# The first four units of each stage on gain times z instead of on the normalised x, their products ordered by feature block

## The reference

```
h = layer_norm(ALPHA * h + 0.5 * swiglu_ffn(h, w_in, w_out), gain, bias)
h = layer_norm(ALPHA * h + mix(h), gain, bias)
h = layer_norm(ALPHA * h + 0.5 * swiglu_ffn(h, w_in, w_out), gain, bias)

layer_norm(x) = (x - mean(x)) * rsqrt(var(x) + eps) * gain + bias     # over the 1024 features
swiglu_ffn(h) = (silu(h @ w_gate) * (h @ w_up)) @ w_out               # d_ff = 2816
```

## Time and profile before

| | us |
|---|---|
| median of 3 runs | 1088.29 |
| lowest and highest | 1086.24, 1088.48 |
| span of the profiled execution, first to last instruction | 1086.3 |
| TensorE (PE) busy | 1063.5 |
| VectorE (DVE) busy | 693.0 |
| ScalarE (ACT) busy | 510.1 |
| GpSimd (POOL) busy | 178.2 |

### The profile page before, as it was taken

The page is one execution under the profiler, slowest core; times in us unless marked ns, Lnnn a source line. Parts: engine busy times, 40 slices in busy tenths (PEclk is TensorE's granted clock), DMA queues, the critical chain, the costliest instruction groups (busy, mean ns, idle before and its releaser), DMA issues.

```text
span 1086.3 us, 21913 instructions
## 1 busy us (share of the span) xinstructions
PE 1063.5 (98%) x8293; PEld 1035.4 (95%) x8293; DVE 693.0 (64%) x972; ACT 510.1 (47%) x737; POOL 178.2 (16%) x188
## 2 busy tenths in 40 slices
PE   7999999999999999999999999999999999999996
PEld 6999999989999999999899999997998989999995
DVE  5755556588788555565676565658545877666664
ACT  5434344463347343444553434447745665434442
POOL 4000002230062000012400000223131460000032
PEclk9999999999999999999999999999999999999998
DMA  9756555627564765556285555562632528665531
GB/s 260 213 174 173 168 167 169 192 81 213 174 173 113 200 174 173 161 174 183 85 231 175 173 168 161 176 172 81 178 98 78 153 84 242 182 191 170 173 103 40
DMA packets 343692, 175.14 MB, mean 161 GB/s; under 512 B 6658, under 2 KB 342576, under 8 KB 343632
## 3 DMA queue, kind: packets, MB, share of 16 engines
q1 hardware_dynamic: 342992, 173.36, 55.9%
q10 hardware_dynamic: 448, 0.85, 0.2%
q0 software_dynamic: 192, 0.10, 0.0%
HBM read 173.24 MB, written 1.05 MB: 160 GB/s over the span
## 4 chain that ended last, share of the span: by engine, by line
PE 94%; DVE 4%; ACT 1%; DMA 1%; issue 0%; POOL 0%; SPq 0%; DVEq 0%; POOLq 0%; ACTq 0%
PE bank L1089 28%; PE bank L1091 28%; PE bank L1090 28%; PE bank L1109 2%; PE bank L1113 2%; PE bank L1110 2%; DVE rstd L791 1%; DMA raw_weights<-in_ffn_w_in_dram 1%; PE bank L1304 1%; PE bank L1321 1%; DVE scaled L800 1%; DVE weights_lo L734 0%; DVE resid L788 0%; PE bank L1131 0%; PE bank L1317 0%
## 5 line engine op out<-in xcount | busy, mean ns | idle before, releaser
L734 DVE TENSOR_TENSOR weights_lo<-raw_weights,weights_hi 128x1024 fp32r<-128x1024 f32 x335 | 424.8, 1274 | 247.2 <-ACT weights_hi L437 246.4
L437 ACT ACTIVATE weights_hi<-raw_weights 128x1024 fp32r<-128x1024 f32 x337 | 355.2, 1059 | 451.9 <-PE bank L1091 443.9
L1089 PE MATMUL bank<-x_hi,weights_hi 128*128 128x272 f32 (+1 forms) x1640 | 474.5, 289 | 0.5 <-DVE yc_lo L941 0.3
L1091 PE MATMUL bank<-x_hi,weights_lo 128*128 128x272 f32 (+1 forms) x1640 | 472.6, 288 | 0.0
L1090 PE MATMUL bank<-x_lo,weights_hi 128*128 128x272 f32 (+1 forms) x1640 | 471.0, 287 | 0.0
L1089 PEld LDWEIGHTS bank<-x_hi,weights_hi 128*128 128x128 f32 x1640 | 310.4, 189 | 4.5 <-issue 3.5
L1091 PEld LDWEIGHTS bank<-x_hi,weights_lo 128*128 128x128 f32 x1640 | 310.6, 189 | 0.0
L1090 PEld LDWEIGHTS bank<-x_lo,weights_hi 128*128 128x128 f32 x1640 | 310.5, 189 | 0.0
L1089 PE MATMUL bank<-mid_hi,weights_hi 128*128 128x272 f32 (+1 forms) x704 | 201.3, 286 | 0.0
L1091 PE MATMUL bank<-mid_hi,weights_lo 128*128 128x272 f32 (+1 forms) x704 | 201.1, 286 | 0.0
L1090 PE MATMUL bank<-mid_lo,weights_hi 128*128 128x272 f32 (+1 forms) x704 | 200.9, 285 | 0.0
(11 more groups left out here) (169 smaller groups left out, 897.8 us busy)
## 6 DMA issues: line engine op xcount, KB each, us to landing
raw_weights<-in_ffn_w_in_dram SPq DMA_DIRECT2D x176, 512.0 KB, 3.9
raw_weights<-in_ffn_w_out_dram SPq DMA_DIRECT2D x64, 512.0 KB, 4.0
raw_weights<-in_ffn_w_out_dram SPq DMA_DIRECT2D x32, 384.0 KB, 3.4
raw_weights<-in_conv_w_in_dram SPq DMA_DIRECT2D x24, 512.0 KB, 3.9
raw_weights<-in_gla_w_in_dram SPq DMA_DIRECT2D x24, 512.0 KB, 3.8
raw_weights<-in_conv_w_out_dram SPq DMA_DIRECT2D x8, 512.0 KB, 4.0
raw_weights<-in_gla_w_out_dram SPq DMA_DIRECT2D x8, 512.0 KB, 4.0
out_dram<-out_tok SPq DMA_DIRECT2D x3, 256.0 KB, 2.2
```

The lines of the kernel that those rows point to most:

```text
L437: nc.scalar.activation(w_hi[:, n % RING, :], raw[:, n % RING, :], ACT.Copy).then_inc(hi_split, 1)
L734: nc.vector.tensor_tensor(w_lo[:, s, :], raw[:, s, :], w_hi[:, s, :].bitcast(F32), ALU.subtract).then_inc(lo_split, 1)
L1089: nc.tensor.matmul(ps, w_h, hi[:, k, cols], start=first and k == k0, stop=False)
L1091: mm = nc.tensor.matmul(ps, w_l, hi[:, k, cols], start=False, stop=last and k == k1 - 1)
```

## The change

The first four units after a norm (FOLD = 4) no longer use the norm's output, except in f0, which has no norm in front. They multiply `zg = gain * z`, split into zg_hi (ScalarE, `round_raw`) and zg_lo (VectorE, `raw_low`) chunk by chunk during the out-projection. Two more columns of zg hold gain and bias, so each bank also receives w.gain and w.bias. After the norm's statistics VectorE turns each of the four banks into `unfolded` (`unfold`), and the consumer adds `fold_bias`. The mean products stand inside the four units, before block 2. The 96 products run over the blocks outside and the four units inside. `keep_warm` is gone from the boundaries. VectorE's `scaled` is written back into resid and h_f is no longer used for x; all eight residual blocks are made on ScalarE (`take_residual`), all eight are centred on GpSimd. One low split of weights goes between block 5 and 6 of the normalising loop, and in f2 to gla the unfolding of unit 0 goes between block 1 and 2 (`early`). The fifth unit waits for `xlo_ready` block by block.

```diff
+            def round_raw(q, mo, n_tok, step=0):
+                nc.scalar.activation(zg_hi[:, at, cols], resid[:, at, cols], ACT.Identity,
+                                     scale=gain_at(q, step * 2 + mo)).then_inc(zghi_ready, 1)
+            def take_residual(q, k, n_tok):
+                act.wait_ge(xlo_ready, KD * (q + 1) + k + 1)
+                nc.scalar.activation(resid[:, k, cols], resid[:, k, cols], ACT.Identity, scale=ALPHA,
+                                     bias=alpha_bias[:, q * KD + k:q * KD + k + 1]).then_inc(resid_ready, 1)
...
+            def raw_low(q, mo, n_tok, step=0):
+                dve.wait_ge(zghi_ready, step * 2 + (KD * q + mo + 1))
+                nc.vector.scalar_tensor_tensor(out=zg_lo[:, at, cols], in0=resid[:, at, cols],
+                                               scalar=gain_at(q, step * 2 + mo), in1=zg_hi[:, at, cols].bitcast(F32),
+                                               op0=ALU.mult, op1=ALU.subtract).then_inc(zglo_ready, 1)
+            def unfold(q, n0, u, n_tok):
+                dve.wait_ge(unit_used, n0 + u + 1)
+                nc.vector.scalar_tensor_tensor(out=unfolded[:, u, cols], in0=mean[:, cols], scalar=ps[:, n_tok:n_tok + 1],
+                                               in1=ps[:, 0:n_tok], op0=ALU.mult, op1=ALU.subtract,
+                                               reverse1=True).then_inc(fold_step, 1)
+                nc.vector.tensor_copy(fold_bias[:, u:u + 1], ps[:, n_tok + 1:n_tok + 2])
+                dve.wait_ge(fold_step, FOLD * q + u + 1)
+                nc.vector.tensor_tensor(unfolded[:, u, cols], unfolded[:, u, cols], rstd[:, cols],
+                                        ALU.mult).then_inc(fold_ready, 1)
...
+                    if k >= 1:
+                        x_low(k - 1)
+                    if k == 1 and early is not None:
+                        early()
+                    if k == 5:
+                        split_lo(late + RING)
...
+                    unfold(q, n0, 0, n_tok)
+                    unfold(q, n0, 1, n_tok)
+                    split_lo(n0 + RING)
+                    gate_times_up(0)
+                    split_lo(n0 + 1 + RING)
+                    unfold(q, n0, 2, n_tok)
+                    unfold(q, n0, 3, n_tok)
+                    split_lo(n0 + 2 + RING)
+                    gate_times_up(1)
+                    split_lo(n0 + 3 + RING)
...
+            def multiply_raw(n0, q, n_tok):
+                for u in range(FOLD):
                     pe.wait_ge(lo_split, n0 + u + 1)
-                keep_warm(n0, WARM[1])
-                pe.wait_ge(var_ready, q + 1)
-                keep_warm(n0, WARM[2])
-                pe.wait_ge(std_ready, q + 1)
-                keep_warm(n0, WARM[3])
+                pe.wait_ge(fold_cols, 4 * (q + 1))
                 for k in range(KD):
+                    if k == 2:
+                        mean_total(q, n_tok)
+                        mean_squares(q, n_tok)
+                    pe.wait_ge(zglo_ready, KD * q + k + 1)
+                    for u in range(FOLD):
+                        ps = bank[u][:, 0:n_tok + 2]
+                        nc.tensor.matmul(ps, w_h, zg_hi[:, k, cols], start=k == 0, stop=False)
+                        nc.tensor.matmul(ps, w_h, zg_lo[:, k, cols], start=False, stop=False)
+                        mm = nc.tensor.matmul(ps, w_l, zg_hi[:, k, cols], start=False, stop=k == KD - 1)
                         if k == KD - 1:
                             mm.then_inc(unit_used, 1)
+                pe.wait_ge(mean_copied, q + 1)
+                pe.wait_ge(var_ready, q + 1)
...
             for j in range(GLA_TILES):
+                if 0 < j < FOLD:
+                    unfold(FFN_NORM[2], n0, j, T)
                 if j < GLA_TILES - 1:
                     split_lo(n0 + j + RING)
```

More of the change, by code:

```diff
@@ L492, in normalise, with out_projection @@
                     act.dma_start(out[0, P:, D // 2:], out_tok[:, 1, D // 2:]).then_inc(out_stored, 16)
-            def out_projection(q, n0, parts, n_tok):
+                else:
+                    for k in range(KD - 2, KD):
+                        take_residual(q, k, n_tok)
+            def out_projection(q, n0, parts, n_tok, early=None):
                 def chunk(mo, step=0):
@@ L811, in normalise, with out_projection @@
                     x_low(KD - 1)
-                for n in late:
-                    split_lo(n + RING)
-            def out_projection(q, n0, parts, n_tok):
+            def out_projection(q, n0, parts, n_tok, early=None):
                 def chunk(mo, step=0):
@@ L946, in conv_chunk @@
                 split_lo(n + RING, step)
+                if m == 0:
+                    for u in range(1, FOLD):
+                        unfold(FFN_NORM[0], n0, u, T)
                 convolve(m, step)
                 split_lo(n + 2 + RING, step)
+            unfold(FFN_NORM[0], n0, 0, T)
             conv_chunk(0)
@@ L1187, in ffn @@
                 else:
-                    multiply_together([bank[b][:, 0:n_tok] for b in range(4)], n0, q)
+                    multiply_raw(n0, q, n_tok)
                 if q is None:
                     pe.wait_ge(consts_ready, 1)
-                tile(2)
+                tile(2, ready=None if q is None else (xlo_ready, KD * (q + 1)))
                 tile(3)
@@ L1228, in _ @@
             every = slice(0, T)
[L1229 removed]
+            multiply_raw(n0, FFN_NORM[0], T)
             def conv_chunk(m, step=0):
@@ L1234, in conv_chunk @@
                 for part in range(1 if m == 1 else 0, 3):
-                    multiply(bank[3 * (m % 2) + part][:, 0:T], n0 + 3 * m + part, (x_hi, x_lo), every, step=step)
+                    multiply(bank[3 * (m % 2) + part][:, 0:T], n0 + 3 * m + part, (x_hi, x_lo), every, step=step,
+                             ready=(xlo_ready, KD * (FFN_NORM[0] + 1)) if m == 1 and part == 1 else None)
             conv_chunk(1)
@@ L1347, in _ @@
                 cols = main if short else every
-                multiply(bank[j % 2][:, 0:SEQ if short else T], n0 + j, (x_hi, x_lo), cols)
+                multiply(bank[j % 2][:, 0:SEQ if short else T], n0 + j, (x_hi, x_lo), cols,
+                         ready=(xlo_ready, KD * (FFN_NORM[2] + 1)) if j == 4 else None)
                 if j == 4:
```

298 lines of the change are left out of this document (186 added, 112 removed).

## The result

The changed kernel takes 1094.41 us (median of 4 runs, 1093.54 to 1094.82), the kernel before beside it 1088.11 us (4 runs). The ratio is 1.0059, with a 95% interval of 1.0046 to 1.0071: slower by 0.6%. The forecast was 1092.1, slower. The profiled execution has a span of 1092.7 us against 1086.3.

What follows compares the result with a forecast made beforehand. TensorE, busy 1063.5 of 1086.3 us, bounds the kernel, so only its pauses can be won. Terms +3.5 - 2.0 - 2.9 + 6.4 - 1.2 = +3.8 us, added to the 1088.29 median, give 1092.1 us; range 1081 to 1100.

Steps and rivals of the forecast that it cites:

- What is removed: At five norm boundaries: 18 warming products and the norm wait go; four units end at +12.9 instead of +19.1 us.
- VectorE up to the last x block: After a norm, VectorE's scaled blocks and low parts, partly slowed beside GpSimd's centring, deliver block 7 at +17.2 us.
- the first rival: In the sixteen normalising instructions, GpSimd's centring does not hold VectorE: block 7 at +15.1, kernel 1080 us; chance 0.22.
- The first tile: At f1 to f2, the third pair waits for the first gate-times-up: TensorE restarts at +22.2, before +25.1; 2.9 us gained.
- Conv: At f0 to conv, the third chunk waits for yc_lo until +27.6: 1.9 us lost, plus 1.6 of low clock, 3.5 together.
- gla: At f2 to gla, VectorE's wait for unit 0 and unit-by-unit copies and splits lose 6.4 us; bounds 0 and 10.
- The ping-pong of 3.6 us: In gla, units 1 to 3 each take unfold, kT copy, high split and low split in turn, 3.6 us a unit.
- The signs named: New-trace TensorE waits: x_lo 1 to 2 us, mid_lo 1.5, yc_lo near 7, kT near 4; low clock behind conv, gla.
- the 20 below which I would have been wrong: Refutation test: the forecast is wrong if TensorE's waits for VectorE and ScalarE sum to less than 20 us.
- the boundaries behind stages with one unit per block: Conv to f1 and gla to f3: raw_low adds 0.42 to 0.75 us per block; 2.0 and 1.2 us gained.
- the 23.1 and 22.7 of the sum: Forecast TensorE restarts, in us after +0, at conv to f1 and gla to f3, with gains of 2.0 and 1.2.
- The rival with the clock in the feed-forward stages: At the feed-forward boundaries the clock falls too, costing 3 x 1.6 us and the port's 1.4 more: 1098; chance 0.16.

Runs made afterwards that it cites:

- the unit order: The 96 raw products unit by unit instead of block by block: 1095.55 us against the changed kernel's 1094.41; on top of the four changes of order, 1082.65 us.
- the last experiment but one: Changed kernel with four changes of order together (gla unfoldings, conv convolution, late split, early unfolding), plus the 96 products unit by unit: 1082.65 us, ratio 0.9952.
- the first: Changed kernel with only the 96 products unit by unit instead of block by block, mean products after the first unit: 1095.55 us, ratio 1.0077.

## Why the prediction was right

**What is removed.** The raw products start 0.12 us after the last out-projection product at all five boundaries, and at f1 to f2 the four units end near +13.1, forecast +12.9. Right.

**VectorE up to the last x block.** Forecast +17.2, measured +17.4, and GpSimd's centring ends at +11.2 for a forecast of +11.3. Of the durations, three instructions beside GpSimd took 1.02 instead of the 0.85 of the earlier trace rows, and the undisturbed ones followed each other every 0.41 instead of 0.43; the two nearly cancel. Without the centring the last block came at +15.5, where the first rival had +15.1, and the restarts in front of conv and the feed-forward stages moved by the 2 us that it named. The rival priced the disturbance at these four restarts rightly and was wrong that it would be absent. Its 1080 us asked for more: in gla the restart did not move (+33.11), and the slow clock in conv stayed (238.06 to 244.89), so that the run stands at 1087.2.

**The first tile.** Forecast +22.2, measured +22.3, with VectorE's wait for SiLU of 0.61 inside.

**Conv.** Forecast +27.6 and 3.5 lost; measured +27.4 and 3.7. Of this the clock is 1.8 by the run with warming products (forecast 1.6) and the queue of VectorE the other 1.9. With its convolution ahead of the splits the restart comes 2.7 us sooner, though with the slow clock again.

**gla.** Forecast: wait of 2.5, block 7 at +19.6, j=6 at +32.5, cumulative products at +48.1, 6.4 lost. Measured: 2.53, +20.2, +33.1, +48.5, 6.7. The ping-pong of 3.6 us was right, and taking it apart gave 5.1 of the 6.7 back. The clock's part was not as forecast. I named 1.6 us of slow clock behind a wait of near 4 us for kT. The wait is 1.77, as the clock was at 0.50 from 753.4 to 763.7, through the logits and into the unit behind them, which filled the pause; with the clock kept up the wait is 2.69 and j=6 starts no sooner. The slow clock behind the wait came (767.1 to 770.5) but cost nothing that shows, as the wait for qT took it up.

**The signs named.** TensorE's waits were shorter than named: 0.8 to 1.5 for x_lo, 1.2 to 1.3 for mid_lo, 6.2 for yc_lo. Their sum with those for kT, qT and the total is 23 us, or 20.4 without the total, which the kernel before waited for too; this is only just above the 20 below which I would have been wrong.

**Where 2.3 us were missed.** In the profiled spans it is 2.6 us. The largest term, 1.2, is the boundaries behind stages with one unit per block. What was mis-sized there is the price of the raw low part, 1.00 where I had 0.42 to 0.75; the cycle from z to z still came out at the 3.2 that I took (mostly 2.78 and 3.58 in turn), which is luck, since the split took 1.21 instead of 1.79 in two of six blocks. The restarts at +23.4 and +22.95 are 0.3 later than the 23.1 and 22.7 of the sum, and the old restarts were 0.1 sooner than I had worked out. Another 0.35 us of the 1.2 is lost in the out-projection of f3: without any wait, its products start 0.1186 us apart instead of 0.1180. This shows in the other traces with the fold too; its cause is open. Another 0.6 came before the first boundary, where the change does little: in the traces of the experiments that point lies anywhere from 215.65 to 216.60, so I take it for scatter from one execution to the next. Conv and gla were 0.2 and 0.3 worse than forecast, f1 to f2 0.3.

**The rival with the clock in the feed-forward stages** (1098) did not come: their waits are up to 1.3 us and the clock stays at 1.00. It came in the unit order, at conv to f1, so it is near.

## What to carry to other kernels

In this kernel, work taken out of TensorE's wait was only won where the engine that makes the next operand was through sooner too: VectorE's busy time grew by 44 us (693.0 to 736.7), and each restart was set by the place of an instruction in that list. After such a change, read at every restart which engine was last, and move each split or copy that nobody waits for behind the one that is waited for or into an idle stretch ahead of it: four such moves turned +0.6% into -0.6% without changing an operation. Refill a pause with warming products only where TensorE itself is last afterwards: it gave 1.8 and 1.5 us in the conv stretch and nothing in gla.

## What the runs showed of the hardware that was not expected

GpSimd and VectorE both lose when they run side by side: a low part of 0.49 us took 1.02, a split of 1.21 took 1.80, and GpSimd's own addition went from 0.97 to 1.75. Without GpSimd's centring the changed kernel is 7.2 us shorter by the medians and 8.1 by the traces, although VectorE never waits for a centred block.

The granted clock fell to 0.50 after two waits of 0.87 and 0.6 us with 0.65 us of products between them, but not after waits of 0.85 and 1.2 us with several us of products between, in the feed-forward stages. In gla it fell at 753.43 in the changed kernel, behind waits of 1.47 and 1.32 us; of the two us from 751 to 753 TensorE was busy for 0.65. In the last experiment but one it held at gla to f3 behind the same two waits with which it had fallen in the first, so these runs give cases and no rule.
